# Row vectors of the second block's layer norms: spread over partitions by TensorE into PSUM in place of eight broadcast loads

## What is computed

```python
def _layer_norm(x, g, b):
    mu = jnp.mean(x, axis=-1, keepdims=True)
    var = jnp.mean(jnp.square(x - mu), axis=-1, keepdims=True)
    return (x - mu) * lax.rsqrt(var + 1e-5) * g + b

for l in range(2):                      # x: 256 tokens x 1024
    mix = (sum over 4 branches of gate * proj) @ w_out
    x = _layer_norm(alpha * x + mix, ln1_g, ln1_b)
    x = _layer_norm(alpha * x + peer_ffn(x), ln2_g, ln2_b)
```

## Time and profile before

| | |
|---|---|
| median of 3 runs | 2794.36 us (2794.36 to 2795.07) |
| the profiled execution's own time | 2793.43 us |
| its span, first to last instruction | 2791.6 us |
| busy: PE, DVE, ACT, POOL | 2289.3, 1352.1, 1298.8, 742.2 us |
| moved by DMA | 839.32 MB |
| of it gathers | 536.90 MB |
| mean granted clock of TensorE | 0.900 |

### The profile page before, as it was taken

The page is one execution under the profiler, slowest core; times in us unless marked ns, Lnnn a source line. Parts: engine busy times, 40 slices in busy tenths (PEclk is TensorE's granted clock), DMA queues, the critical chain, the costliest instruction groups (busy, mean ns, idle before and its releaser), DMA issues.

```text
span 2791.6 us, 33734 instructions
## 1 busy us (share of the span) xinstructions
PE 2289.3 (82%) x13336; PEld 1937.5 (69%) x13336; DVE 1352.1 (48%) x3183; ACT 1298.8 (47%) x2327; POOL 742.2 (27%) x614
## 2 busy tenths in 40 slices
PE   8989998999999995887886888687688797666666
PEld 7878887886875875876765877566687675555554
DVE  3652332321002233775546665545766555686444
ACT  2751113100000221586746567754568774666665
POOL 0021012100000001333333323333323333335553
PEclk9989999999999997998997999998898998777666
DMA  6221121133443765999999999999999999999997
GB/s 250 111 91 61 67 78 46 54 115 141 154 152 150 266 249 216 420 421 414 411 420 417 421 421 420 409 420 421 414 420 421 412 403 422 415 385 358 421 421 316
DMA packets 110142, 839.32 MB, mean 301 GB/s; under 512 B 12192, under 2 KB 12576, under 8 KB 14112
## 3 DMA queue, kind: packets, MB, share of 16 engines
q0 software_dynamic: 73728, 536.90, 46.8%
q1 hardware_dynamic: 36256, 300.25, 27.2%
HBM read 836.06 MB, written 1.05 MB: 300 GB/s over the span
## 4 chain that ended last, share of the span: by engine, by line
PE 48%; DMA 23%; ACT 12%; DVE 11%; issue 4%; POOL 2%; SPq 0%; POOLq 0%; DVEq 0%; ACTq 0%
DMA mem<-in_puv,mem 21%; PE psm L445 10%; PE psm L2249 6%; PE psm L453 5%; PE psm L1812 4%; PE psm L758 4%; DVE mem L2293 4%; ACT mem L2267 4%; PE psm L1353 3%; PE psm L2124 3%; PE psm L1456 3%; PE psm L2011 2%; ACT L2262 1%; PE psm L1504 1%; PE psm L449 1%
## 5 line engine op out<-in xcount | busy, mean ns | idle before, releaser
L2249 PE MATMUL psm<-mem 128*128 128x128 f32 x4096 | 669.2, 318 | 351.7 <-ACT mem L2267 349.3
L2277 POOL DMA_INDIRECT mem<-in_puv,mem x512 | 619.4, 1210 | 978.5 <-PE psm L2249 906.7
L2249 PEld LDWEIGHTS psm<-mem 128*128 128x128 f32 x4096 | 556.9, 165 | 461.2 <-ACT mem L2267 441.9
L2293 DVE CUSTOM_DVE_ANT_0 mem<-mem 128x1024 f32<-128x1024 f32 x512 | 623.8, 1224 | 445.4 <-DMA mem<-in_puv,mem 438.6
L2267 ACT ACTIVATE mem<-mem 128x1024 f32<-128x1024 f32 x512 | 588.9, 1150 | 16.7
L445 PE MATMUL psm<-mem 128*128 128x256 f32 (+2 forms) x1376 | 313.8, 391 | 3.1 <-DVE mem L1293 1.5
L445 PEld LDWEIGHTS psm<-mem 128*128 128x128 f32 x1376 | 262.3, 193 | 53.5 <-issue 14.8
L2262 ACT ACTIVATE mem<-mem 128x1 f32<-128x1 f32 x512 | 101.7, 199 | 407.6 <-DVE mem L2293 405.3
L1812 PE MATMUL psm<-mem 128*128 128x256 f32 x1024 | 252.9, 395 | 0.5 <-ACT mem L1532 0.5
L453 PEld LDWEIGHTS psm<-mem 128*128 128x128 f32 x1440 | 187.5, 196 | 49.3 <-issue 21.6
L453 PE MATMUL psm<-mem 128*128 128x128 f32 x1440 | 199.6, 283 | 22.7 <-DVE mem L1128 6.9
(11 more groups left out here) (364 smaller groups left out, 2368.7 us busy)
## 6 DMA issues: line engine op xcount, KB each, us to landing
mem<-in_w2g SPq DMA_DIRECT2D x64, 1024.0 KB
mem<-in_w SPq DMA_DIRECT2D x18, 2048.0 KB, 8.3
mem<-in_pwq SPq DMA_DIRECT2D x32, 1024.0 KB
mem<-in_w2f SPq DMA_DIRECT2D x28, 1024.0 KB
mem<-in_wgu SPq DMA_DIRECT2D x11, 2048.0 KB, 7.9
mem<-in_w2t SPq DMA_DIRECT2D x20, 1024.0 KB
mem<-in_w2b SPq DMA_DIRECT2D x16, 1024.0 KB
mem<-in_w2o SPq DMA_DIRECT2D x16, 1024.0 KB
```

The source lines that it names most:

```text
L2249: m = pe.matmul(bank(6 + c // 4)[:, tsl(c % 4)], GR[n % PING][:, 1024 + c * 128:1152 + c * 128], ident, is_transpose=True, start=k == 0 an ...
L2277: po.indirect_dma_start(GR[n % PING], None, A[f"puv{i // 2}"], bass.IndirectOffsetOnAxis(ap=IX[i % 2][:, k:k + 1], axis=0)).then_inc(gsem[ ...
L2293: ve.tensor_tensor_reduce(out=GR[n % PING][:, 0:1024], in0=GR[n % PING][:, 0:1024], in1=X[:, i % 2, :], scale=1.0, scalar=0.0, op0=MUL, op ...
```

## The change

The eight loads `ga` and `gf` are taken out of `uses`. One load of 32 KB puts the four rows of both layers into an SBUF area of constants that the second block doesn't use: 16 partitions x 512 numbers, partition `4 * row + part`. A matmul whose stationary operand is column `k` of a 16 x 16 identity, read 128 times, writes partition `k` of that table to all 128 partitions of a PSUM bank. Four such matmuls give gain and bias. They stand in two of the steps of `mix_pe` and `fin_pe` that were empty, DVE waits for them, and its multiply and add read PSUM.

```diff
+        ROWS = CST[0:16, off[0] - 7 * 128:off[0] - 3 * 128]
...
-                    mix=[("b", n, 2 * n + 2, 2 * n + 3) for n in R4] + [("o", n, 12 + n, 12 + (n | 1)) for n in R4] + [("ga", 0, 19, 21)],
-                    query=[("q", n, 4 * n, 8 * (n // 2) + 7) for n in R8], fin=[("gf", 0, 8, 9)])
+                    mix=[("b", n, 2 * n + 2, 2 * n + 3) for n in R4] + [("o", n, 12 + n, 12 + (n | 1)) for n in R4],
+                    query=[("q", n, 4 * n, 8 * (n // 2) + 7) for n in R8])
...
+        def row_pe(pe, b, row, part):
+
+            k = 4 * row + part
+            return pe.matmul(bank(b), ident[0:16, k:k + 1].broadcast_to((16, 128)), ROWS, start=True, stop=True)
...
         def mix_pe(pe, i):
...
-            for _ in R6:
+            pe.wait_ge(rt_sem, 16)
+            for b, part in ((4, 0), (5, 1), (2, 2), (3, 3)):
+                m = row_pe(pe, b, i // 2 * 2, part)
+                if part % 2 == 1:
+                    if part == 3:
+                        m.then_inc(BP.next((i, "b")), 1)
+                    yield
+            for _ in R4:
                 yield
...
         def mix_ve(ve, i):
...
-            ve.wait_ge(*landed2("ga", i, 0))
-            ve.tensor_tensor(x, x, gb[:, 0:1024], MUL).then_inc(ov.up(), 1)
+            ve.wait_ge(*BP[i, "b"])
+            ve.tensor_tensor(x, x, psm[:, 2048:3072], MUL).then_inc(ov.up(), 1)
             yield
             ve.wait_ge(*ov.now())
-            ve.tensor_tensor(x, x, gb[:, 1024:2048], ADD).then_inc(BV.next((i, "l")), 1)
+            ve.tensor_tensor(x, x, psm[:, 1024:2048], ADD).then_inc(BV.next((i, "l")), 1)
...
         def fin_ve(ve, i):
...
-            ve.wait_ge(*landed2("gf", i, 0))
+            ve.wait_ge(*PP[i, "b"])
             ve.wait_ge(*ov.now())
-            ve.tensor_tensor(x, x, gb[:, 0:1024], MUL).then_inc(ov.up(), 1)
+            ve.tensor_tensor(x, x, psm[:, 2048:3072], MUL).then_inc(ov.up(), 1)
             yield
             ve.wait_ge(*ov.now())
-            ve.tensor_tensor(x, x, gb[:, 1024:2048], ADD).then_inc(PV.next((i, "l")), 1)
+            ve.tensor_tensor(x, x, psm[:, 0:1024], ADD).then_inc(PV.next((i, "l")), 1)
...
         def fin_pe(pe, i):
...
-            for _ in R8:
+            if i < 3:
+                pe.wait_ge(*BV[i + 1, "l"])
+            for b, part in ((4, 0), (5, 1), (0, 2), (1, 3)):
+                m = row_pe(pe, b, i // 2 * 2 + 1, part)
+                if part % 2 == 1:
+                    if part == 3:
+                        m.then_inc(PP.next((i, "b")), 1)
+                    yield
+            for _ in R6:
                 yield
...
             sp.dma_start(SW2, A["sw2"][0, :, :]).then_inc(sm_sem, 16)
+            sp.dma_start(ROWS, A["rows"][2:6, :].rearrange("r (c n) -> (r c) n", n=512)).then_inc(rt_sem, 16)
```

More of the change, by code:

```diff
@@ L342, in build @@
         p_sem, k_sem = sem("p"), sem("k")
-        sm_sem, ky_sem = sem("sm"), sem("ky")
+        sm_sem, ky_sem, rt_sem = sem("sm"), sem("ky"), sem("rt")
         gsem = [sem(f"g{i}") for i in range(PING)]
@@ L411, in build @@
         BP = marks("b_p", [(i, x) for i in RI for x in [("t", 0), ("t", 1), *[("w", j) for j in R8], ("m", 0), ("m", 1),
-                                                        ("o", 1), ("o", 3), ("h", 0), ("h", 1)]])
+                                                        ("o", 1), ("o", 3), "b", ("h", 0), ("h", 1)]])
         BV = marks("b_v", [(i, x) for i in RI for x in [("t", 0), *[("w", j) for j in R4], ("x", 0), *[("w", j) for j in range(4, 8)],
@@ L421, in build @@
         EP, EA, EV = [marks(n, range(NE)) for n in ("e_p", "e_a", "e_v")]
-        PP = marks("p_p", [x for i in RI for x in [(i, "y0"), (i, "y1")] + [(i, c) for c in R2 if i < 2]])
+        PP = marks("p_p", [x for i in RI for x in [(i, "y0"), (i, "y1"), (i, "b")] + [(i, c) for c in R2 if i < 2]])
         PV = marks("p_v", [(i, x) for i in RI for x in ["y", "x0", "x1", "st", "l"] + ["h"] * (i < 2)])
@@ L438, in build @@
             freed2 |= {("b", i, n): BP[i, ("w", 2 * n + 1)] for n in R4} | {("o", i, n): BP[i, ("o", n // 2 * 2 + 1)] for n in R4}
-            freed2 |= {("ga", i, 0): BV[i, "l"], ("gf", i, 0): PV[i, "l"]} | {("q", i, n): WP[i, n // 2] for n in R8}
+            freed2 |= {("q", i, n): WP[i, n // 2] for n in R8}
         def chain(pe, o, lhs, rhs, ks, start=True, stop=True):
@@ L2057, in mix_ve @@
             st, mv, v = ln_parts(t)
-            gb = slot2(("ga", i, 0), 2048)
             ve.wait_ge(*BP[i, ("t", 0)])
@@ L2301, in fin_ve @@
             t = i % 2
-            gb = slot2(("gf", i, 0), 2048)
             st, mv, v = ln_parts(t)
@@ L2471, in source2 @@
                 return A["cmpw"][L, :, :]
-            if n in ("ga", "gf"):
-                r = 2 + 2 * L + (n == "gf")
-                return A["rows"][r:r + 1, :].broadcast_to((128, 2048))
             return A[dict(f="w2f", g="w2g", b="w2b", o="w2o", q="pwq")[n]][L, m, :, :]
```

## The result

| | before | changed |
|---|---|---|
| median, us (lowest to highest) | 2794.65 (2794.36 to 2795.07), 4 runs | 2809.22 (2805.55 to 2811.78), 4 runs |
| profiled execution, us; its span | 2793.43; 2791.6 | 2808.23; 2806.4 |
| records of matmuls and transposes on PE in the profile | 13336 | 13400 |

The ratio is 1.0052 (1.0038 to 1.0067): **slower by 14.6 us**, where 13 us faster was forecast, and outside the range of 2774 to 2789 us. L1980 is the row matmul, L2113 and L2340 are the multiplies that read it.

What follows compares the result with a forecast made beforehand. It took DMA throughput (about 421 GB/s) as the bound from 1103 to about 2440 us and from about 2560 us, routing work between. 2793.43 − 14.94 + 1.72 = 2780.2, plus 0.93 for the median: 2781 us, range 2774 to 2789.

Steps and rivals of the forecast that it cites:

- item 6: On PE: 24 row matmuls between expert transposes, 4 before, 4 after; mostly hidden, +1.72 us exposed (0 to 3.44).
- item 1: DMA-bound part: six removed 1 MB loads, 2.49 us each, give 14.9 us in full.
- Items 2 to 5: Loads at 1044.7 and 2460.8 us, 32 KB table, SP's order: each taken as 0.
- Item 6, the price: Row matmuls on PE: 0.43 us each, four cost 1.72 us, or 3.44 us at low clock.
- Item 6, the final norms of tiles 0 and 1: Row matmuls among query projections: slip absorbed by gathers landed under a full DMA; zero, at worst 1.72 us each.
- Item 6, the final norm of tile 2: Row matmuls on the serial routing chain at 2437.63 us, no DMA cover: +1.72 us (bounds 0 and 3.44).
- Item 6, after the last expert: Kernel's end: four rows done by 2782.9 us (low clock 2784.6), before DVE's multiply at 2785.41; hidden.
- Item 6, the mixes: Row matmuls at the mixes of tiles 0 to 3: hidden in PE's idle time; without cover in tiles 1 to 3, 1.72 us each.
- Item 7: DVE's multiply and add read rows from PSUM: 0 for all 16; skill's rule would add about 0.3 us.
- Item 8: DVE's multiply waits for PE instead of a DMA; PE is 2 to 5 us ahead, so no real wait.
- PE becomes the bound at its lower clock: Rival: 24 row matmuls among the experts, none hidden, 0.86 us each: +5.7, 2800 us; chance 5%.
- list of signs: Wrong if DMA rate falls at same length, DVE waits for PE, or transposes lag and POOL's PE waits grow 10 us or more.

Runs made afterwards that it cites:

- e5: Changed kernel with final-norm row matmuls moved behind expert steps 121 and 124 of their own tile and all row matmuls contracting over 128 partitions: 2782.24 us, ratio 0.9954.
- e3: Changed kernel with row matmuls contracting over all 128 partitions instead of 16, same places: 2795.32 us, ratio 0.9993 to before.
- e4: Changed kernel, still 16 rows, with each final norm's row matmuls moved ahead behind expert steps 121 and 124 of their own tile: 2784.36 us, ratio 0.9956.
- e1: Changed kernel without any row matmuls, loads still gone; DVE does like operations with constants in SBUF, leaving out gain and bias: 2786.07 us, ratio 0.9957.
- e6: Changed kernel with 16-row matmuls only at the mixes; final norms get their 1 MB loads back and have no row matmuls: 2792.94 us, ratio 0.9981.
- e8: Changed kernel with row matmuls contracting over 64 partitions instead of 16: 2796.57 us, ratio 1.0004 to before.
- e7: e2 with row matmuls contracting over 128 partitions instead of 16: 2802.6 us, ratio 1.0024 to before.
- e2: Changed kernel with the eight loads back and DVE reading rows from them, all 32 row matmuls and their waits kept: 2821.82 us, ratio 1.0082.

## Why the prediction was wrong, point by point

The step that failed is item 6, what the row matmuls cost: their price was half of what it is, their place in the final norms of tiles 0 and 1 and at the end was taken for hidden, and no term had what the clock does. The gain of item 1 held. The runs give the sum that stands in place of mine, in ratios against before. From e5 to e3, which differ only in the place of the final norms' row matmuls, 0.0039 or 10.9 us; from e3 to the changed kernel, which differ only in the rows that are contracted over, 0.0059 or 16.5 us; e5 itself is at −12.9 us. −12.9 + 10.9 + 16.5 = +14.5. The sum must come out, since its terms are steps between measured kernels; it says how the loss splits on this way from e5, each step uncertain by some 5 us. On the other way, rows first, the number of rows is worth 0.6 us once the row matmuls are moved (e4 to e5) and their place is worth 26.8 us (changed to e4). Cost of place and cost of rows are not independent.

- **Item 1, six loads for 14.9 us:** right in kind, perhaps a little too high. 12.0 (e1), 12.3 (e4) and 12.9 us (e5), each of them with all eight loads gone. 14.9 lies inside the intervals of e1 and e5, so the runs don't show that it was too much.
- **Items 2 to 5** (the two loads outside the DMA-bound part, the small table, SP's order): zero, and nothing contradicts it. e1 has all four and gains, but none was tried alone.
- **Item 6, the price: wrong by a factor of two.** I took 0.43 us for a matmul, from 16 records in 6.88 us, and multiplied by matmuls of the *program*. But a float32 matmul stands as two records. The earlier trace rows held it: the 64 matmuls that L1995 issues stand there as x128. At the full clock the four cost 8 × 0.43 = 3.44 us, not 1.72, and that is just how much longer the ruler is in e3 (10.58 against 7.14).
- **Item 6, the final norms of tiles 0 and 1, "zero": wrong in place.** I argued that the DMA is full across the passage, so gathers that landed meanwhile take up a slip. But a gather is issued only when PE's transposes have freed its buffer, and these stand behind the row matmuls on the same queue. The reserve ran out: in tile 1 the DMA share fell to 0.83 and 0.52. They lost 5.4 and 9.3 us. Even at the full clock (e3) these two passages lose 3.0 and 3.4 us, more than nothing; of tile 0's some is not the matmuls', as e1 loses 2.4 us there without any.
- **Item 6, the final norm of tile 2, +1.72 (0 to 3.44):** the place was right and the mechanism too: transposes, query matmuls, ACT's copies, DVE. The loss there was 9.3 us, and 4.7 in e3.
- **Item 6, after the last expert, "hidden": wrong.** By my price the rows would be done 0.8 us ahead of DVE's multiply even at the low clock. With two records for each matmul at that clock they take 7.19 us; DVE waits 3.19 us, and the tail is 3.9 us longer (1.6 in e3). In both, 1.6 us come from the last two groups of transposes ahead of the row matmuls, which ran at the lower level (1.97 us each instead of 1.10 and 1.09). e1 has them too, without any row matmul, so they are not the row matmuls' doing; the 3.19 us of DVE's wait are.
- **Item 6, the mixes, "hidden": held,** even at twice the price (e5 can't be told from e1, and e6 gains). This is the row of tile 0, after (PE, DVE):

```profile
1060.05 4.72 PE L1980 MATMUL psm<-mem 16*128 16x512 f32 x8
1064.88 1.22 DVE L2113 TENSOR_TENSOR mem<-mem,psm 128x1024 f32<-128x1024 f32 x1 [0.80 <-PE psm L1980]
```

- **What no item had:** that the new matmuls could move the clock of what stands around them. I had two prices for two clocks, but took which one held from the trace of before, where these passages ran at 1.00. This is the largest term: 16.5 us from e3 to the changed kernel, of which 13.4 us (e8 to the changed kernel) go with the clock.
- **Item 7, PSUM:** zero, held: 1.22 us for 1024 columns. The estimate from the Trainium skill ("VectorE: DVE Perf Modes", TRN2 errata) of 0.065 us more per instruction is not borne out by that row, which takes as long as the same multiply from SBUF, nor by e1, which reads SBUF and is no faster than e5.
- **Item 8, waits:** nothing at the mixes but 0.8 us in tile 0; a real one at the end.
- **The rival "PE becomes the bound at its lower clock"** had the sign and the engine, at 5%. It named the expert stretch as a whole with 0.86 us a matmul. In fact the losses lie in the three final norms and the tail, with up to 1.8 us a matmul and slowed neighbours.

The forecast's list of signs did work: PE's routing matmuls late behind L1980, and POOL's waits for PE grown by 16 us (906.7 to 923.0), which that list has under "wrong".

What stays open: *why* few rows go with the lower clock. e3, e7 and e8 against the changed kernel and e2 show that the number of rows decides in these passages; e4 shows that the place does too, and with 16 rows two passages of six kept the full clock. Nothing between 16 and 64 rows was tried, nor other contents in the added rows, so rows and the data in them aren't told apart. Of the 10.9 us of the place, the three stretches by the ruler give 3 × 3.44 = 10.3 us, which is PE's own work; that the DMA running dry behind them costs anything on top was not shown.

## What to carry to other kernels

Before you price a new instruction by a record of the trace, divide that group's records by the instructions that the program issues: here the two differ by a factor of two for float32 matmuls, and not for transposes. A full DMA is no cover for work that is put ahead of the very instructions that free its buffers; look for what *issues* the transfers, and place fill-in work where no serial chain over three engines begins, as e4 did at no cost that shows. Where a table has few rows, try the contraction over the whole partition range with zeros in the selector (it gained in both pairs where the row matmuls stood in the final norms, and nothing that shows where they were moved), and look at the granted clock of the passage, not only of the kernel, which moved by just 0.01 here.

## What the runs showed of the hardware

- A float32 matmul of 512 columns stands as two records and passes in 0.86 us at the full clock over 128 rows (e3); a transpose stands as one. Over 16 or 64 rows it is no shorter but a little longer: four records take 1.91 us to the next matmul instead of 1.73 (changed, e8, e3), and the stretch with eight of them 11.35 and 11.36 us instead of 10.58.
- In two of the three final norms PE was busy 92 to 100% with 16-row matmuls among the work, and its granted clock was 0.79, 0.73 and (e2) 0.62; with 128 rows in the same places it was 1.00. The whole kernel differs by 16.5 us (0.6%) for it, or 16.2 with the loads in. Over 64 rows the clock was 1.00 too (e8).
- The lower level outlasts them: eight records of query matmuls over 128 rows, behind the row matmuls, took 2.08 us instead of 1.05 (changed, e3).
- VectorE's multiply of 1024 columns took 1.22 us with one input in PSUM (changed, tile 0) and 1.22 us with both in SBUF (before).
